# A two-layer attention trunk in float32: tiles 0 and 1 of x turned as loaded in the first layer, their norm carried by channel behind the turn and by row in q, k, v and z

## What is computed

```
def rms_norm(x, g):
    return x * rsqrt(mean(x * x, axis=-1) + 1e-6) * g

for i in range(2):
    hdn = rms_norm(x, norm_g[i])
    q, k, v, z = split(hdn @ w_in[i], 4)          # layer 1 has forget logits too
    q, k = rms_norm(q, q_norm), rms_norm(k, k_norm)   # per head; layer 0 also turns them by position
    y = causal_attention(q, k, v)                 # layer 1 with the sums of log forget gates
    x = x + (y * silu(z)) @ w_out[i]
```

## Time and profile before

| | |
|---|---|
| median of three runs | 551.37 us (550.82 to 551.73) |
| the profiled execution | 549.96 us, its span 547.7 us |
| PE busy | 540.7 us (99%), 2966 products |
| DVE, ACT, POOL busy | 407.8 us (74%), 286.7 us (52%), 294.1 us (54%) |
| granted clock of PE | 1.00 over the span |
| chain that ended last | PE 98%, transfers 1% |

### The profile page before, as it was taken

How to read it: one execution, slowest core, us unless ns; L and a number is a source line. 1 busy time by engine, 2 the same in 40 slices (tenths; PEclk the granted TensorE clock), 3 DMA queues, 4 the chain that set the end, 5 groups by cost and what they waited for, 6 DMA issues and landing times.

```text
span 547.7 us, 9735 instructions
## 1 busy us (share of the span) xinstructions
PE 540.7 (99%) x2966; PEld 499.0 (91%) x2966; DVE 407.8 (74%) x1023; ACT 286.7 (52%) x841; POOL 294.1 (54%) x348
## 2 busy tenths in 40 slices
PE   6999999999999999999999999999999999999997
PEld 4999999999999999888888999999999999998887
DVE  3777899999999999963563758787777777779331
ACT  5737373838383838372445483837373737464400
POOL 5864544545454546352745485857474747476300
PEclk9999999999999999999999999999999999999999
DMA  9813313131313121223413345425141534132121
GB/s 267 241 35 93 108 58 97 58 98 57 96 57 96 57 96 66 87 94 109 121 34 79 96 99 77 114 60 133 41 133 41 127 51 126 67 110 71 40 96 59
DMA packets 78236, 49.94 MB, mean 91 GB/s; under 512 B 4089, under 2 KB 71417, under 8 KB 78210
## 3 DMA queue, kind: packets, MB, share of 16 engines
q1 hardware_dynamic: 78208, 49.61, 33.2%
q10 hardware_dynamic: 2, 0.00, 0.0%
HBM read 47.48 MB, written 2.11 MB: 91 GB/s over the span
## 4 chain that ended last, share of the span: by engine, by line
PE 98%; DMA 1%; SPq 0%; DVE 0%; ACT 0%; issue 0%
PE banks L345 27%; PE banks L347 27%; PE banks L346 27%; PE banks L468 6%; PE banks L454 3%; PE banks L443 2%; PE banks L442 2%; PE banks L441 2%; PE banks L377 1%; DMA first_raw<-in_a_w_in_dram 1%; PE banks L494 0%; PE banks L495 0%; PE banks L426 0%; SPq L299 0%; DVE hT_lo L816 0%; SPq L259 0%
## 5 line engine op out<-in xcount | busy, mean ns | idle before, releaser
L1085 POOL TENSOR_TENSOR w_lo<-w_raw,w_hi 128x512 fp32r<-128x512 f32 x147 | 189.8, 1304 | 85.1 <-ACT w_hi L604 85.1
L345 PE MATMUL banks<-w_hi,hT_hi 128*128 128x384 f32 x512 | 173.4, 339 | 1.8 <-DVE hT_lo L816 1.8
L347 PE MATMUL banks<-w_hi,hT_lo 128*128 128x384 f32 x512 | 171.5, 335 | 0.0
L346 PE MATMUL banks<-w_lo,hT_hi 128*128 128x384 f32 x512 | 171.5, 335 | 0.0
L873 DVE STREAM_TRANSPOSE banks<-qkn 32x256 f32<-32x256 f32 x240 | 109.4, 456 | 3.3
L345 PEld LDWEIGHTS banks<-w_hi,hT_hi 128*128 128x128 f32 x512 | 96.5, 188 | 3.0 <-POOL w_lo L1085 2.1
L346 PEld LDWEIGHTS banks<-w_lo,hT_hi 128*128 128x128 f32 x512 | 96.5, 188 | 0.6
L347 PEld LDWEIGHTS banks<-w_hi,hT_lo 128*128 128x128 f32 x512 | 96.3, 188 | 0.0
L604 ACT ACTIVATE w_hi<-w_raw 128x512 fp32r<-128x512 f32 x148 | 89.2, 638 | 8.9 <-PE banks L347 5.4
L640 ACT ACTIVATE junk<-banks 128x128 bf16<-128x128 f32 x128 | 33.8, 270 | 87.3 <-PE banks L347 87.3
L1101 POOL TENSOR_TENSOR msq<-ssq,eps 128x2 f32<-128x2 f32 x64 | 12.8, 200 | 118.0 <-ACT junk L640 117.7
(11 more groups left out here) (110 smaller groups left out, 893.0 us busy)
## 6 DMA issues: line engine op xcount, KB each, us to landing
w_raw<-in_b_w_in_dram SPq DMA_DIRECT2D x64, 256.0 KB, 3.7
w_raw<-in_a_w_in_dram SPq DMA_DIRECT2D x52, 256.0 KB, 2.8
w_raw<-in_w_out_dram SPq DMA_DIRECT2D x32, 256.0 KB, 2.6
first_raw<-in_a_w_in_dram SPq DMA_DIRECT2D x12, 256.0 KB, 5.5
cos_t<-c_rows SPq DMA_DIRECT2D x8, 256.0 KB, 3.5
out_dram<-xs SPq DMA_DIRECT2D x7, 256.0 KB, 2.1
xs<-in_x_dram SPq DMA_DIRECT2D x3, 512.0 KB, 5.8
xs<-in_x_dram SPq DMA_DIRECT2D x2, 256.0 KB, 2.9
```

The source lines that it names most:

```text
L345: pe.matmul(dst, ah, bh, start=first and m == 0, stop=False)
L346: pe.matmul(dst, ah, bl, start=False, stop=False)
L347: mm = pe.matmul(dst, al, bh, start=False, stop=last and m == n - 1)
L1085: pool.tensor_tensor(w_lo[:, slot, k, :], raw, f32(w_hi[:, slot, k, :]), ALU.subtract).then_inc(wlo_set, by)
```

## The change

For tiles 0 and 1 of layer 0 (`UNSCALED = 2`):

- TensorE turns x itself. The norm's gain is loaded as 8x128, turned to a column per chunk (`turn_gain`) and multiplied in as the turned chunk is split. All four tiles of layer 0 are split in pieces of one chunk, with that factor as a scale; tiles 2 and 3 are still scaled by row before the turn.
- The row's root goes where the products come out: v gets it as the scale of its split, q and k through an epsilon multiplied by the mean square, z by a new VectorE step per head (`scale_z`) over its first 256 columns, with the roots as a row on every partition. That row comes by a store to DRAM and a load back (SP).
- The squares of tiles 0 and 1 and their roots move behind the weights; `scale_gain` moves behind the norm of tile 3; `exp_z` of layer 0 moves from the end of a period to behind `exps` of the next.
- SP issues weight chunk 0 behind the first half of tile 0, chunk 1 behind the second, chunks 2 to 5 behind tile 1, then tile 2, chunks 6 and 7, tile 3. TensorE turns tile 2 whole ahead of chunk 6.

Core of the diff:

```diff
@@ SP, at the end of load_second and then in the opening order
+                sp.wait_ge(rawrs_set, UNSCALED)
+                sp.dma_start(r_rows, r_raw[:, :]).then_inc(r_stored, 16)
+                sp.wait_ge(r_stored, 16)
+                sp.dma_start(r_row[:, :], r_rows.rearrange("p t -> (p t)").partition_broadcast(P)).then_inc(r_in, 16)
...
                 sp.dma_start(xs[:, 0, cols], x[0, 0:P, cols]).then_inc(x_half[half], 16)
+                load_first((half,))
             load_x(1)
-            load_first(range(KC))
+            load_first(range(2, 6))
             load_x(2)
+            load_first((6, 7))
             load_x(3)
@@ TensorE
+            def turn_gain():
+                pe.wait_ge(gain_in[0], 16)
+                pe.transpose(banks[:, GAIN_BANK, 0:KC], gz[0:KC, 0, 0:P], ident[0:KC, 0:KC]).then_inc(gain_turned, 1)
...
+                if unscaled(layer, t):
+                    buf = xs[:, t, :]
+                    pe.wait_ge(x_half[half] if t == 0 else x_in[t], 16)
...
                     for k in range(3, KC):
-                        if k == KC - 1:
-                            turn_half(layer, 2, 0)
+                        if k == 6:
+                            turn_hidden(layer, 2)
                         first_w(0, k)
                         qkv_part(layer, 0, 0, 0, (k,))
                         qkv_part(layer, 0, 0, 1, (k,))
-                    turn_half(layer, 2, 1)
@@ ScalarE
+                if layer == 0:
+                    for c in range(4):
+                        k = 4 * half + c
+                        act.activation(hT_hi[:, k, t * P:(t + 1) * P],
+                                       turned(t, k), ACT.Copy, scale=gain_col[:, k:k + 1]).then_inc(rawhi_set, 1)
...
+                    act.activation(v_hi[:, s, t, :], v, ACT.Copy, scale=r_raw[:, t:t + 1]).then_inc(vhi_set, 1)
...
-                act.wait_ge(z_done, g + 1)
+                act.wait_ge(z_done if layer else zr_set, g + 1)
...
-                    for half in range(2):
-                        square_half(half)
-                    square_x(layer, 1)
-                    split_w(layer, 0, 0, (0, 1))
-                    split_hidden(layer, 0)
+                    act.wait_ge(gain_set, 1)
+                    split_w(layer, 0, 0, (0,))
+                    split_half(layer, 0, 0)
+                    split_w(layer, 0, 0, (1,))
+                    split_half(layer, 0, 1)
                     split_w(layer, 0, 0, (2,))
                     split_hidden(layer, 1)
                     split_w(layer, 0, 0, (3, 4, 5))
                     square_x(layer, 2)
                     split_w(layer, 0, 0, (6, 7))
+                    square_x(layer, 0)
                     square_x(layer, 3)
                     split_hidden(layer, 2)
+                    square_x(layer, 1)
                     read_qkv(layer, 0, 0, 0)
@@ ScalarE, in period
                 exps(layer, h)
+                if layer == 0:
+                    exp_z(layer, h)
                 split_w(layer, h + 2, s, (2,))
@@ VectorE
+                        dve.scalar_tensor_tensor(out=hT_lo[:, k, t * P:(t + 1) * P],
+                                                 in0=turned(t, k),
+                                                 scalar=gain_col[:, k:k + 1], in1=f32(hT_hi[:, k, t * P:(t + 1) * P]),
+                                                 op0=ALU.mult, op1=ALU.subtract).then_inc(rawlo_set, 1)
...
+                    dve.tensor_scalar(buf[:, cols], xs[:, t, cols], ssx[:, t, 1:2], None, ALU.mult).then_inc(xn_set, 1)
...
+            def scale_z(layer, h):
+                if isinstance(h, int) and h == 0:
+                    dve.wait_ge(r_in, 16)
+                dve.wait_ge(z_done, HEADS * layer + h + 1)
+                part = banks[:, Z_BANK, 0:UNSCALED * P].rearrange("p (t n) -> p t n", n=P)
+                dve.tensor_tensor(part, part, r_row[:, :].rearrange("p (n t) -> p t n", t=UNSCALED), ALU.mult).then_inc(zr_set, 1)
...
                     norm_x(layer, 2)
                     split_first_w(0, (7,))
-                    scale_gain()
                     split_hidden(layer, 2)
                     norm_x(layer, 3)
+                    scale_gain()
@@ VectorE, in period and in last
                 maxima(layer, h)
+                if layer == 0:
+                    scale_z(layer, h)
...
                 begin(layer, h)
+                if layer == 0:
+                    scale_z(layer, h)
@@ Pool
+                if unscaled(layer, t):
+                    pool.tensor_tensor(eps_raw[:, t, :], msx[:, t:t + 1].broadcast_to([P, 2]), eps[:, :],
+                                       ALU.mult).then_inc(epsraw_set, 1)
...
-                    rstd_x(layer, 0)
-                    rstd_x(layer, 1)
                     for k, by in POOL_FIRST.items():
                         if k == 6:
                             rstd_x(layer, 2)
                         split_w(layer, 0, 0, (k,), by=by)
-                    rstd_x(layer, 3)
+                    for t in (0, 3, 1):
+                        rstd_x(layer, t)
                     pool.wait_ge(tables_set, 1)
```

More of the change, by code:

```diff
@@ L24 @@
 RAW = 4
+UNSCALED = 2
 EPS = 1e-6
@@ L606, in square_x @@
             def square_x(layer, t):
+                if layer == 1:
+                    act.wait_ge(x_added, TILES * OUT_CHUNKS * layer - TILES + t + 1)
+                elif t == 0:
+                    for half in range(2):
+                        act.wait_ge(x_half[half], 16)
+                else:
+                    act.wait_ge(x_in[t], 16)
+                if unscaled(layer, t):
+                    if t == 3:
+                        act.wait_ge(rawsq_set, 1)
+                    squares = (pT_hi, pT_lo, probs, pT_hi)[t][:, 0:DM]
+                    act.activation(squares, xs[:, t, :], ACT.Square, scale=DM ** -0.5,
+                                   accum_out=ssx[:, t, 0:1]).then_inc(rawsq_set, 1)
+                else:
+                    act.activation(hT_hi[:, :, t * P:(t + 1) * P], xs[:, t, :].rearrange("p (k n) -> p k n", k=KC),
+                                   ACT.Square, scale=DM ** -0.5, accum_out=ssx[:, t, 0:1]).then_inc(xsq_set, 1)
@@ L607, in square_x, with split_hidden, split_half @@
+            def split_hidden(layer, t):
+                for half in range(2):
+                    split_half(layer, t, half)
+            def split_half(layer, t, half):
                 n = TILES * layer + t
+                act.wait_ge(hT_turned, 2 * n + half + 1)
                 if layer == 0:
-                    act.wait_ge(x_in[t], 16)
-                else:
-                    act.wait_ge(x_added, TILES * OUT_CHUNKS * layer - TILES + t + 1)
-                act.activation(hT_hi[:, :, t * P:(t + 1) * P], xs[:, t, :].rearrange("p (k n) -> p k n", k=KC),
-                               ACT.Square, scale=DM ** -0.5, accum_out=ssx[:, t, 0:1]).then_inc(xsq_set, 1)
@@ L633, in read_qkv @@
+                    return
+                act.activation(hT_hi[:, 4 * half:4 * half + 4, t * P:(t + 1) * P],
+                               banks[:, turn_bank(layer, t) + half, :].rearrange("p (k n) -> p k n", k=4),
+                               ACT.Copy).then_inc(hThi_set, 1)
             def read_qkv(layer, h, s, t):
@@ L729, in first @@
                 split_w(layer, 1, 1, (6, 7))
-                exp_z(layer, 0)
+                if layer == 1:
+                    exp_z(layer, 0)
             def begin(layer, h):
@@ L754, in period @@
                 split_w(layer, h + 2, s, (6, 7))
-                exp_z(layer, h + 1)
+                if layer == 1:
+                    exp_z(layer, h + 1)
             def last(layer):
@@ L812, in split_half @@
             def split_half(layer, t, half):
-                n = TILES * layer + t
-                dve.wait_ge(hThi_set, 2 * n + half + 1)
+                if layer == 0:
+                    for c in range(4):
+                        k = 4 * half + c
+                        together = 4 if t else 2
+                        if k % together == 0:
+                            dve.wait_ge(rawhi_set, KC * t + k + together)
+                        dve.scalar_tensor_tensor(out=hT_lo[:, k, t * P:(t + 1) * P],
+                                                 in0=turned(t, k),
+                                                 scalar=gain_col[:, k:k + 1], in1=f32(hT_hi[:, k, t * P:(t + 1) * P]),
+                                                 op0=ALU.mult, op1=ALU.subtract).then_inc(rawlo_set, 1)
+                    return
+                dve.wait_ge(hThi_set, 2 * t + half + 1)
                 dst = slice(4 * half, 4 * half + 4), slice(t * P, (t + 1) * P)
```

156 lines of the change are left out of this document (86 added, 70 removed).

## The result

| | before | after |
|---|---|---|
| median | 551.64 us (550.82 to 552.41, 5 runs) | 555.35 us (554.43 to 555.82, 5 runs) |
| ratio to before | | 1.0064 (95% interval 1.0049 to 1.008) |
| profiled execution, its span | 549.96 us, 547.7 us | 555.47 us, 553.5 us |

What follows compares the result with a forecast made beforehand. TensorE's work almost alone was taken to bound the kernel. Profiled 549.96 us + 0.5 (start) + 1.2 (layer 0 loop) = 551.7, as a median 551.37 + 1.7 = 553.1 us; own range 552.0 to 554.5, wider range 550.2 to 555.0.

Steps and rivals of the forecast that it cites:

- The likeliest case: Whole kernel: slower through a later start and a longer layer 0 loop, 553.1 us (552.0 to 554.5), chance 0.4.
- term 1: Start of layer 0: the fourth norm comes late, turn of q and k at 38.0 instead of 37.5, +0.5 us.
- term 2: Layer 0's heads: the moved exponent makes the loop 27.28 us, 0.23 over TensorE's period, using up slack at the scores; +1.2 us.
- The walk to the z projection: Start: first product near 6.5 us, 4.1 earlier; z projection near 30.3 instead of 32.04, 1.7 us left.
- early-start rival: Start: faster small copies, tables begin by 21.3, turn of q and k 1.7 us early; 549.7 us, chance 0.2.
- The norms that wait for Pool: Start: tile 2's norm waits 1.0 us for Pool's chunk 6, delaying tables by up to 1.0; 554.1 us, chance 0.15.
- Costed at nothing: Start: roots' trip to memory on SP ahead of the forget weights costs nothing, 0.5 us at most if ScalarE is held.

Runs made afterwards that it cites:

- e4: Kernel before with only layer 0's exponent of z moved behind the exps of the next period: 552.96 us, ratio 1.0045.
- e2: Changed kernel with tile 1's square and root ahead of tile 3's and the q gain scaled between the halves of tile 2's split: 552.14 us, ratio 1.0032.
- e5: Changed kernel with z's scaling moved ahead of the maxima and its exponent behind weight chunk 0: 553.36 us, ratio 1.0034.
- e9: Changed kernel unedited, run again on one chip beside the kernel with filler transposes: 554.5 us, ratio 1.0064.
- e7: Changed kernel with earlier tables, z steps and forget weights, plus a one-column activation loading the activation table early: 550.35 us, ratio 0.9988.
- e8: Kernel before with one unread VectorE product of z's 128x256 behind the maxima of layer 0's heads but the last: 551.41 us, ratio 1.0005.
- e10: Kernel before with eight unread VectorE products ahead of the first head's fourth norm: 554.63 us, ratio 1.0067.
- e6: Changed kernel with both the earlier tables and earlier z steps, and forget weights loaded ahead of the roots' trip to memory: 550.12 us, ratio 0.9982.
- e3: Changed kernel without the scaling of z and with its exponent back at the end of a period: 553.7 us, ratio 1.0049.
- e11: Changed kernel with 20 unread identity transposes ahead of the turn of q and k, repeated beside the unedited changed kernel: 553.87 us, ratio 1.0051.
- e1: Changed kernel with 20 unread identity transposes between the z projection and the first head's turn of q and k: 554.23 us, ratio 1.0067.

## Why the prediction was wrong

The likeliest case had the right sign and the right two places, and both terms were too small. The sum was made for the profiled execution, 551.7 us; that of the changed kernel took 555.47. The last scores of that execution are 5.87 us later than those of before: 3.20 from the start, where term 1 had 0.5; 2.27 from the loop of layer 0, where term 2 had 1.2; and 0.40 behind the loop.

The medians are only 3.7 us apart. The forecast put its median 1.4 above the profiled execution, as it was before; in the changed kernel it lies 0.1 below. The profiled execution of before was an early one. That step hid 1.5 of the 3.8 us by which the sum was short, which is luck, and 2.3 were left.

In the ratios the loop is 1.0045, +2.5 us, by e4, which has nothing else, and 1.0032, +1.8, by what e2 leaves. The start is 1.0034, +1.9 us, by what e5 leaves. Each is known to about 0.7 us by its interval. With 2.2 to 2.3 us for the loop in all profiles that have it, 1.2 to 1.4 of the 3.5 to 3.7 are left for the start and the rest.

**Term 1, the turn of q and k: the first step that failed.** Its wait was forecast at 2.2 us and measured at 2.37, for the fourth norm, as said. Two things were mis-sized.
- The turn was to be at 38.0 and was at 39.07. The table products began at 24.00 instead of 23.5: the square of tile 1 ended 0.3 later, and Pool's epsilon sum, root and product behind it took 1.5 us instead of 1.2. From there to the turn it was 15.07 us, not 14.5: up to the fourth epsilon sum Pool took 11.84 us, as forecast (11.85), but that sum took 0.65 us, 0.73 with the step to the root, where 0.24 was put in. The trace of before had 0.44 there, and 0.52 with the step.
- The wait was priced as delay alone. Behind it the clock was at 0.50 for about 3.4 us (an estimate from the four windows). The profiles put that at 1.4 to 1.66 us, and executions of one kernel with and without it lie 0.9 us (e9) to 2.0 us (e5) apart. In the changed kernel they are 1.0 apart, three of five had it, and so it is 0.6 us in their mean.

**What made Pool's small operations long.** The prediction asked whether VectorE waits for Pool, and not whether Pool waits for VectorE. The kernel before, where VectorE subtracts two SBUF tensors:

```profile
32.45 0.87 DVE L824 TENSOR_TENSOR w_lo<-w_raw,w_hi 128x512 fp32r<-128x512 f32 x1
32.94 0.44 POOL L1101 TENSOR_TENSOR msq<-ssq,eps 128x2 f32<-128x2 f32 x1 [0.16 <-ACT junk L640]
```

In the thirteen profiles 41 of Pool's epsilon sums began while VectorE was in such a subtraction or in a tensor_scalar from SBUF to SBUF. They took 0.36 to 0.65 us, and each ended 0.05 us after VectorE's operation. The other 891 took 0.18 to 0.22. In the changed kernel the sum at 22.50 ended at 22.99, behind the first half of tile 3's norm (22.94), the root at 23.06 ran beside the second half and took 0.81 us (0.55 for that of tile 3, at 19.72), and the fourth sum ended at 36.49, behind VectorE's 36.44. The three together are 1.0 us longer than undisturbed ones. Against what the forecast had put in for them it is 0.8 of the 1.07 us by which the turn was late. In e2, where no such operation stood beside them, the sum and root of tile 1 took 0.19 and 0.55. No run moved VectorE's subtraction away from the fourth sum.

**The walk to the z projection.** The first product was at 8.16 instead of 6.5. Chunk 0 was there at 4.76 (about 4.5 forecast), but the activation table load, 1.28 us, came only then. Before, it stood at 1.28 us, out of the way; the forecast did not have it. e7 shows that this changes nothing at the end. The eight scaled copies took 2.16 us (2.4 forecast) and the eight on VectorE 2.16 (2.2). TensorE reached the z projection at 31.06 (30.3 forecast). The early-start rival's condition, tables at 21.3 or sooner, did not come true, and that rival falls. e2 shows that TensorE would not have been at the turn early either: with the tables at 22.14, the z projection stands at 32.06, not 30.3. That is where the profile of before has it, and 0.5 to 1.4 us ahead of the profiles of e4, e8 and e10, so a part of the early product may still be a gain, as in e6.

**The norms that wait for Pool.** This rival's mechanism was there: tile 2's two halves took 1.91 us, the first of them 1.51, ending 0.3 behind Pool's chunk 6; tile 3's took 0.88 beside small operations, and in e2 2.25 beside the tables. ScalarE then waited 0.72 us for the turn of tile 2, and the tables came 0.5 later than forecast, half of what the rival said. The Trainium skill (SBUF — State Buffer, "Who interferes with whom") has the lock also for a tensor_scalar in its two-port mode; these rows, which the trace of before did not have, agree. The square of tile 1, which stands behind that wait, ended 0.3 us later than forecast; the other 0.3 is Pool's sum and root above. No run takes the two apart.

**Term 2, the loop: the second step that failed.** The cause held: e4 has the growth from the exponent's place alone, e3 and e5 lose it, and e8's scaling costs nothing, as the 0.41 us idle let expect. The size was off twice. The excess is 0.32 us a head, not 0.23. And the slack was looked for in the wrong place: 1.23 us at the scores, which would have hidden the first four rounds. TensorE meets the same loop first at the values. There the low half of the probabilities was 0.39 us early in head 0 and came 0.91 later, so the weight loads of head 0 wait for 0.59 us already, and no round is hidden. With no slack the forecast's own loop gives 0.41 + 6 x 0.23 = 1.8 us; 2.27 was measured. From head 7 to the last head of layer 1 another 0.40 us was added, where nothing was forecast (5.47 to 5.87); where it came from was not looked into.

**Costed at nothing, rightly for the time.** The forget weights came at 38.05 us and ScalarE waited 5.7 us for them, far more than the 0.5 that was allowed for. e2 has the same order on SP and no wait at the turn, so TensorE did not feel it.

**What stays open.** Why the clock falls behind the same idle stretch in one execution and not in the next; why the price of the fall differs between kernels (0.9 to 2.0 us); whether e6's 0.9 us of gain is the shorter start, as the z projections suggest; and what parts the medians of e9 and e11.

## What to carry to other kernels

Where a chain of other engines closes a loop on the bound engine at several places, look for its slack at each of them, and take the smallest: here 0.4 us at the values and not 1.23 at the scores. Where VectorE and Pool both work from SBUF, ask in both directions which waits for which: a Pool sum of 0.2 us took up to 0.65. A wait put on TensorE in mid-stream is to be priced as its delay plus a spell at the lower clock behind it, as a chance and not as a certainty; a few unread products can fill it. A single profiled execution is not the median: before a difference of 1 us is read from it, look where another kernel with the same start stands. An earlier first product is worth what the next transfer leaves of it, and work moved past a tight step (an exponent, a root) can cost more than the start gives.

## What the runs showed of the hardware

- At the turn of q and k, where the profiles show 2.3 to 2.9 us without a product, TensorE's clock fell from 1.00 to 0.50 in 20 of 34 executions (3 of 5 of after and 2 of 6 of e9, 4 of 5 of e3, 8 of 12 of e5, 3 of 6 of e10), and in none of 10 where the stretch was filled (e1, e11). The 0.50 itself is seen in the profiles of after, e3 and e9; the others are counted by a mean clock of 0.997 or less.
- The activation table load (1.28 us) can stand ahead of or behind the wait for the first data: it began at 1.28 us in the kernel before and at 4.76 us in the changed one, when the data was there. A one-column activation at the head of ScalarE's program moved it to 1.36.
- A half of a VectorE tensor_scalar norm (128x512, SBUF to SBUF) took 0.48 us beside small Pool operations, 1.51 when it began behind the start of Pool's chunk 6, and 0.84 and 1.49 beside Pool's table products (e2).
- It goes the other way as well. Pool's sums of one or two columns took 0.18 to 0.22 us (891 of them in thirteen profiles), and 0.36 to 0.65 us when they began while VectorE was in a subtraction of two SBUF tensors or in a tensor_scalar from SBUF to SBUF (41 of 41, each ending 0.05 us behind VectorE's operation).
